# Two norms with their squares summed on VectorE first, and two attention exponentials issued half a chunk later

## The chip, the cores and the metric

The kernel runs on one core of a Trainium2 chip. The metric is the time of one execution on the device in microseconds (us). The engines of the core are TensorE (PE for its matmuls, PEld for its weight loads), VectorE (DVE), ScalarE (ACT), GpSimd (POOL) and SyncE (SP), which here only issues the weights' DMAs. Each engine works through its own list of instructions in order, and they meet at semaphores: an instruction can wait until a semaphore has reached a number, and another raises it when it ends.

## The reference

Two models of width 1024 run one after the other on 256 positions, all in float32. What the change touches is the second (an adaptive-norm block with attention, then one with a short convolution):

```python
def second_block(x, c, ...):                       # cut
    for i in range(2):
        mod = silu(c) @ w_ada[i] + b_ada[i]        # six vectors: shift, scale and gate, twice
        h = rms_norm(x, norm_mix[i]) * (1 + sc_m) + sh_m
        y = moba_attention(h, ...) if i == 0 else short_conv(h, ...)
        x = x + g_m * y
        h = rms_norm(x, norm_ffn[i]) * (1 + sc_f) + sh_f
        x = x + g_f * ((silu(g) * u) @ w_down[i])  # g, u = split(h @ w_gate_up[i])
```

`rms_norm` divides each position by the root of the mean of its 1024 squares (plus 1e-6). The attention has 8 heads of 128 channels; with 256 positions it is plain causal softmax attention, with normed queries and keys.

## The kernel before

The residual stream stands in `res`, transposed: 8 tiles of 128 channels by 256 positions. Every product of a weight and an activation is made of three fast fp32r matmuls (high half by high half, high by low, low by high), in `products` (L1726 to L1728). So each weight unit (128x1024) is first split: ACT copies it rounded to `w_hi` (L597), DVE subtracts to get `w_lo` (L1033), and PE waits for `lo_ready`. Weights come in chunks of two units; the lists of ACT and DVE hold the splits about two chunks ahead of PE's use of them, and between the splits the other work of the stage. The order of all lists is written out by hand in the code; there is no scheduler.

**The second attention** (PE list at c = 0 to 11 for the query, key and value chunks `QKV` + c; c = 12 to 15 are the output projection's chunks `OUT2` + 0 to 3). Beside each half chunk (c, h) stands a piece of the attention, by tables of slots. For head s: PE makes the scores, DVE scales and masks them into `logit2` and takes the negated row maximum `nmax` (`SCORES2`, L1609 to L1613), ACT takes the exponential into `prob2` (L956), DVE multiplies by the reciprocal of the row sum (`weights2`, L1619 and L1621, in DVE's list at the slot of `SCORES2`), PE turns the result over (`PROBS2`, L2224), ACT copies it (L952), and PE multiplies by the values (`VALUES2`, L2235), for which it waits for the copied values too (`v2_ready`, DVE L1632). Also in ACT's list are the squares and the copy of each query or key chunk (`head_squares`, L927 and L929), for which PE's sums of squares wait (`head_sums`, L2204 and L2207), and which wait for the chunk's last matmul.

**The norms before the three up projections** (numbers 1, 3 and 5; before `UP1`, `UP2`, `UP3`, after `OUT1`, `OUT2`, `OUT3`). The last output chunk of the projection runs in two halves on PE: outputs of banks 0 and 1 of four weight rows (then `bank_done`), and the outputs of the other bank, row by row (r = -2, -1, 0, 1). DVE adds the finished banks to `res` (`update`, L1170 and L1178; j = 0 to 3, two tiles each). ACT squares two tiles at a time into `scr` (L606, L621), and PE adds the squares over channels by a plain float32 matmul with ones (`square_part`, L1883): one matmul for each tile, two for each part, parts 0, 1 and 2 between the rows of the last output chunk, parts 3 and 4 in the first up chunk. Meanwhile the first two up chunks already run on the not yet normed activations ("raw", `raw_chunk`, L1797, L1799, L1808), whose two halves ACT (`raw_upper`, L628) and DVE (`raw_lower`, L1124) make. The root of the mean goes through ACT's Ln and Exp (L636, L639) and one Newton step on DVE (L1059 to L1067); the third up chunk (`arriving`, L1763 to L1771) runs on the normed activations (L1072, L650, L1081), and the fourth is the first in steady order.

## Time and profile before

| | us |
|---|---|
| median of 3 runs (lowest, highest) | 910.41 (909.77, 912.11) |
| the profiled execution | 912.87 |
| its span in the trace | 911.3 |
| PE busy | 901.9 (99%) |
| DVE busy | 753.0 (83%) |
| ACT busy | 507.5 (56%) |
| POOL busy | 49.5 (5%) |

The span is the stretch of the trace; the execution's own time is 1.6 us more. A busy share of PE counts matmuls whose ends are modelled and that overlap, so a small wait can hide in it: what PE loses is better seen where two starts in the timeline are further apart than their neighbours. Times in the trace are counted from the start of the span.

### The profile page before, as it was taken

Reading aid. Unit: us, or ns where it says so; the run is one execution under the profiler, and the core shown is the slowest. Engines: PE = TensorE matmul, PEld = TensorE weight load, DVE = VectorE, ACT = ScalarE, POOL = GpSimd, SP = SyncE. Lnnn points to the kernel's source line nnn. Section 1 sums busy time; section 2 is a strip of 40 time slices with the busy share of each in tenths; the row PEclk is TensorE's granted clock in tenths of the full one; section 3 lists DMA queues with packets and bytes.
Section 4 is the critical chain, followed back from the end, with each engine's and each line's share of the span. In section 5 each row is a group of like instructions: output and inputs, shape, how many; then the busy total and the mean of one; then the engine's idle time right before and its main releaser. Section 6 shows DMA issues by size and latency. Waiting matters only on the chain.

```text
span 911.3 us, 18262 instructions
## 1 busy us (share of the span) xinstructions
PE 901.9 (99%) x7351; PEld 877.5 (96%) x7351; DVE 753.0 (83%) x1043; ACT 507.5 (56%) x795; POOL 49.5 (5%) x87
## 2 busy tenths in 40 slices
PE   8999999999999999999999999999999999999998
PEld 8999999999999999999999999999999999999786
DVE  5998989999899799998987887987988887667544
ACT  6456747766665577664754454436554564444531
POOL 5000000000001000010000100100000000000000
PEclk9999999999999999999999999999999999999999
DMA  9887375666667948575379998884677467764541
GB/s 276 288 279 276 106 246 202 215 229 205 230 231 275 327 140 273 171 252 195 127 231 319 323 313 309 314 291 149 201 254 256 135 227 250 239 210 182 184 139 47
DMA packets 132129, 207.72 MB, mean 228 GB/s; under 512 B 4710, under 2 KB 109536, under 8 KB 126944
## 3 DMA queue, kind: packets, MB, share of 16 engines
q1 hardware_dynamic: 123968, 156.47, 51.1%
q0 software_dynamic: 8064, 50.34, 15.9%
q8 instruction: 45, 0.74, 0.3%
q14 instruction: 20, 0.16, 0.1%
q10 hardware_dynamic: 32, 0.01, 0.0%
HBM read 205.75 MB, written 1.05 MB: 227 GB/s over the span
## 4 chain that ended last, share of the span: by engine, by line
PE 86%; DVE 8%; ACT 4%; issue 1%; DMA 1%; SPq 0%; ACTq 0%; DVEq 0%
PE bank L1726 24%; PE bank L1728 24%; PE bank L1727 24%; DVE w_lo L1033 2%; PE bank L1883 2%; PE bank L1799 2%; PE bank L1797 2%; PE bank L1808 2%; PE bank L1771 1%; PE bank L1763 1%; PE bank L1765 1%; ACT w_hi L597 1%; DMA w_raw<-in_w_in 1%; DVE ada_acc L1049 1%; ACT prob L956 1%
## 5 line engine op out<-in xcount | busy, mean ns | idle before, releaser
L1033 DVE TENSOR_TENSOR w_lo<-w_raw,w_hi 128x1024 fp32r<-128x1024 f32 x292 | 351.7, 1221 | 105.7 <-ACT w_hi L597 103.6
L597 ACT ACTIVATE w_hi<-w_raw 128x1024 fp32r<-128x1024 f32 x291 | 304.2, 1056 | 238.2 <-PE bank L1728 220.8
L1726 PE MATMUL bank<-act_hi,w_hi 128*128 128x256 f32 x1296 | 362.2, 279 | 0.1
L1727 PE MATMUL bank<-act_lo,w_hi 128*128 128x256 f32 x1296 | 359.1, 277 | 0.0
L1728 PE MATMUL bank<-act_hi,w_lo 128*128 128x256 f32 x1296 | 359.0, 277 | 0.0
L1727 PEld LDWEIGHTS bank<-act_lo,w_hi 128*128 128x128 f32 x1296 | 244.2, 188 | 0.4 <-issue 0.2
L1726 PEld LDWEIGHTS bank<-act_hi,w_hi 128*128 128x128 f32 x1296 | 243.4, 188 | 0.7 <-issue 0.6
L1728 PEld LDWEIGHTS bank<-act_hi,w_lo 128*128 128x128 f32 x1296 | 243.4, 188 | 0.0
L1049 DVE SCALAR_TENSOR_TENSOR ada_acc<-ada_raw,silu_c,ada_acc 128x2048 f32<-128x2048 f32 (+1 forms) x56 | 114.3, 2041 | 3.6 <-DMA ada_raw<-in_w_ada 3.3
L1726 PE MATMUL bank<-hid_hi,w_hi 128*128 128x256 f32 x352 | 98.2, 279 | 0.0
L1727 PE MATMUL bank<-hid_lo,w_hi 128*128 128x256 f32 x352 | 97.2, 276 | 0.0
L1728 PE MATMUL bank<-hid_hi,w_lo 128*128 128x256 f32 x352 | 97.2, 276 | 0.0
L554 POOL DMA_DIRECT2D ada_raw<-in_w_ada x56 | 29.8, 531 | 737.6 <-DVE ada_acc L1049 730.6
L1726 PEld LDWEIGHTS bank<-hid_hi,w_hi 128*128 128x128 f32 x352 | 66.1, 188 | 0.2
L1727 PEld LDWEIGHTS bank<-hid_lo,w_hi 128*128 128x128 f32 x352 | 66.1, 188 | 0.1
L1728 PEld LDWEIGHTS bank<-hid_hi,w_lo 128*128 128x128 f32 x352 | 66.1, 188 | 0.0
L688 ACT ACTIVATE hid_hi<-hidden 128x512 f32 (+1 forms) x33 | 20.9, 632 | 51.0 <-DVE hidden L1220 49.3
L1726 PE MATMUL bank<-ot_hi,w_hi 128*128 128x256 f32 x128 | 37.4, 292 | 0.0
L1726 PE MATMUL bank<-w_hi,act_hi 128*128 128x256 f32 x128 | 36.9, 288 | 0.0
L1199 DVE SCALAR_TENSOR_TENSOR conv<-bank,vec,conv 128x255 f32<-128x255 f32 (+1 forms) x88 | 35.5, 475 | 0.6 <-ACT conv L668 0.6
L1727 PE MATMUL bank<-w_lo,act_hi 128*128 128x256 f32 x128 | 35.7, 279 | 0.0
L1728 PE MATMUL bank<-w_hi,act_lo 128*128 128x256 f32 x128 | 35.7, 279 | 0.0
(321 smaller groups left out, 1405.5 us busy)
## 6 DMA issues: line engine op xcount, KB each, us to landing
w_raw<-in_w_gate_up SPq DMA_DIRECT2D x44, 1024.0 KB, 5.2
ada_raw<-in_w_ada POOLq DMA_DIRECT2D x40, 1024.0 KB, 5.7
w_raw<-in_w_down SPq DMA_DIRECT2D x33, 1024.0 KB, 6.5
w_raw<-in_w_in SPq DMA_DIRECT2D x23, 1024.0 KB, 6.6
w_raw<-in_w_up SPq DMA_DIRECT2D x22, 1024.0 KB, 5.7
w_raw<-in_w_qkv SPq DMA_DIRECT2D x12, 1024.0 KB, 7.0
w_raw<-in_w_out SPq DMA_DIRECT2D x8, 1024.0 KB, 7.3
ada_raw<-in_w_ada POOLq DMA_DIRECT2D x16, 512.0 KB, 4.5
```

Source lines behind the costliest of these rows:

```text
L554: pool.dma_start(ada_raw[:, j, 0:width], w_ada_2[l][cols(j * P, 2 * P, i, P), s * ADA_W + left:s * ADA_W + left + width]).then_inc(ada_lan ...
L597: act.activation(unit(w_hi, u), raw_half(c, h), ACT.Copy).then_inc(hi_ready, 1)
L688: act.activation(hid_hi[:, cols(2 * p, 4, i, 2), :], hidden[:], ACT.Copy).then_inc(hid_hi_r, 1)
L1033: dve.tensor_tensor(unit(w_lo, u), raw_half(c, h), unit(w_hi, u).bitcast(F32), ALU.subtract).then_inc(lo_ready, 1)
L1049: dve.scalar_tensor_tensor(ada_acc[:, s, part], ada_raw[:, n % 2, 0:width], silu_c[:, k:k + 1], ada_acc[:, s, part], ALU.mult, ALU.add).th ...
L1199: ins = dve.scalar_tensor_tensor(conv[:, q, lag:T], src[:, (q % 2) * T:(q % 2 + 1) * T - lag], vcol(tile, base + f, 4, i), conv[:, q, lag: ...
L1726: pe.matmul(dst, a_hi, b_hi, start=start, stop=False, skip_group_check=True)
L1727: pe.matmul(dst, a_hi, b_lo, start=False, stop=False, skip_group_check=True)
L1728: return pe.matmul(dst, a_lo, b_hi, start=False, stop=stop, skip_group_check=True)
L1797: pe.matmul(dst[t], weights(w_hi, k, t), hi[:, k, 0:width], start=k == 0 and (n > 1 or t == 0), stop=False, skip_group_check=True)
L1799: pe.matmul(dst[t], weights(w_lo, k, t), hi[:, k, 0:width], start=False, stop=False, skip_group_check=True)
L1808: ins = pe.matmul(dst[t], weights(w_hi, k, t), lo[:, k, 0:width], start=False, stop=k == KT - 1, skip_group_check=True)
```

## The change

- For norms 3 and 5, DVE adds the squared tiles before PE sums them: tiles 2 and 3 to tiles 0 and 1, then tiles 4 and 5 to the same (`add_squares`, two 128x512 additions). PE then makes one part of two matmuls in the place of three parts of two; it waits for `sq_added`. Parts 3 and 4 stay.
- ACT squares the three pairs of tiles first and makes most raw upper halves after them.
- DVE's list around these norms: the fold of the modulation for norm 3 (`fold_sum(2)`) and one split of a weight unit stand before the modulation; all eight raw lower halves stand together after the last update; the Newton step takes two instructions on DVE, since ACT makes the mean and the square of the first guess; both splits of the third up chunk stand before the low halves of the normed activations.
- In the second attention ACT takes the exponentials of heads 0 and 3 half a chunk later (`EXPS2`), and at slot (12, 0) its piece of the attention comes before its split.

```diff
+EXPS2 = [(3, 1), (4, 0), (5, 0), (6, 1), (8, 0), (9, 0), (11, 0), (11, 1)]
+PAIRED = (3, 5)
...
                     if raw:
-                        if j == 2 and n not in (2, 4):
+                        if j == 2 and n == 1:
                             split_unit(*late)
...
-                        raw_upper(n, 2 * j)
-                        if (n, j) != (4, 2):
-                            raw_upper(n, 2 * j + 1)
+                        for k in ((), (0,), (1, 2, 3, 4, 5))[j] if n in PAIRED else (2 * j, 2 * j + 1):
+                            if (n, k) != (4, 5):
+                                raw_upper(n, k)
+                            if k == 3 and n in PAIRED:
+                                split_unit(*late)
...
+                if n in PAIRED:
+                    act.activation(n_a[:], bank[SUM_BANK[n]][:, 0:T], ACT.Identity, bias=eps[:], scale=1.0 / D
+                                   ).then_inc(y_mean, 1)
                 act.wait_ge(ln_ready, n)
                 act.activation(n_y[:], n_y[:], ACT.Exp, scale=-0.5).then_inc(y_ready, 1)
+                if n in PAIRED:
+                    act.wait_ge(y_ready, n)
+                    act.activation(n_t[:], n_y[:], ACT.Square).then_inc(y_sq, 1)
...
-                for h in heads_at(SCORES2, c, half):
+                for h in heads_at(EXPS2, c, half):
                     act.wait_ge(m2_ready, h + 1)
...
+                    if (c, h) == (12, 0):
+                        attend2(c, h)
+                        split_unit(QKV + c + 2, h)
+                        continue
...
+            def root(n):
+                if n in PAIRED:
+                    dve.wait_ge(y_mean, PAIRED.index(n) + 1)
+                    dve.wait_ge(y_sq, PAIRED.index(n) + 1)
+                    link(dve.scalar_tensor_tensor(n_t[:], n_t[:], -0.5, n_a[:], ALU.mult, ALU.mult))
+                    link(dve.scalar_tensor_tensor(rstd[:], n_t[:], 1.5, n_y[:], ALU.add, ALU.mult))
+                    return
...
+                if n in PAIRED:
+                    split(c0 + 2)
                 for j in range(4):
-                    if c0 is not None and j % 2 == 0:
+                    if c0 is not None and n not in PAIRED and j % 2 == 0:
                         split_unit(c0 + 2, j // 2)
...
+            def add_up_paired(n, c0, gate, piece):
+                def step(j):
+                    update(bank[OUT_BANKS[c0][j]], j, gate)
+                split_unit(c0 + 4, 0)
+                modulation(piece)
+                dve.wait_ge(unit_done, 2 * (c0 + 2) + 2)
+                step(0)
+                step(1)
+                dve.wait_ge(bank_done, BANKS_DONE[c0] + 1)
+                step(2)
+                add_squares(n, 0)
+                add_squares(n, 1)
+                split_unit(c0 + 4, 1)
+                dve.wait_ge(unit_done, 2 * (c0 + 3) + 2)
+                step(3)
+                raw_lower(n, range(KT))
+                split_unit(c0 + 5, 0)
+
+            def add_squares(n, later_pair):
+                dve.wait_ge(sq_ready, 5 * (n - 1) + 2 + later_pair)
+                if later_pair:
+                    dve.wait_ge(sq_added, 2 * PAIRED.index(n) + 1)
+                pair = slice(2 + 2 * later_pair, 4 + 2 * later_pair)
+                dve.tensor_tensor(scr[:, 0:2, :], scr[:, 0:2, :], scr[:, pair, :], ALU.add).then_inc(sq_added, 1)
...
+                    if (c, h) == (13, 1):
+                        fold_sum(2)
+                        attend2(c, h)
+                        split_unit(QKV + c + 2, h)
+                        continue
...
-            fold_sum(2)
             add_up(OUT2, lambda k: mod[:, 0, G_M + k:G_M + k + 1], 2)
...
-                        if n == 3 and outputs[0] == 2 and r < 1:
+                        if n == 3 and outputs[0] == 2 and r < 1 and NORM_AFTER[c0] not in PAIRED:
                             square_part(NORM_AFTER[c0], r + 2)
+                        if n == 3 and outputs[0] == 2 and r == 0 and NORM_AFTER[c0] in PAIRED:
+                            square_part(NORM_AFTER[c0], 0)
...
-                pe.wait_ge(sq_ready, 5 * (n - 1) + part + 1)
+                if part == 0 and n in PAIRED:
+                    pe.wait_ge(sq_added, 2 * PAIRED.index(n) + 2)
+                else:
+                    pe.wait_ge(sq_ready, 5 * (n - 1) + part + 1)
```

PE's list in the last output chunk of `OUT2`, around the last part of squares ahead of the up projection; first before, then now (`scr` are the squares, `ot_hi` and `ot_lo` the attention's output).

```order
L1728 MATMUL bank<-ot_hi,w_lo 128x256
L1883 MATMUL bank<-scr,ones 128x256 [waits sq_ready]
L1883 MATMUL bank<-scr,ones 128x256
L1726 MATMUL bank<-ot_hi,w_hi 128x256
L1727 MATMUL bank<-ot_lo,w_hi 128x256
```

```order
L1789 MATMUL bank<-ot_hi,w_lo 128x256
L1949 MATMUL bank<-scr,ones 128x256 [waits sq_added]
L1949 MATMUL bank<-scr,ones 128x256
L1787 MATMUL bank<-ot_hi,w_hi 128x256
L1788 MATMUL bank<-ot_lo,w_hi 128x256
```

The place is the same; the two earlier pairs (not shown) are gone, and what this one waits for comes from DVE and no more from ACT.

DVE's list at the same norm, from the second half of the first four updates of `res` on; first before, then now.

```order
L1178 SCALAR_TENSOR_TENSOR res<-bank,mod,res 128x256
L1033 TENSOR_TENSOR w_lo<-w_raw,w_hi 128x1024 [waits hi_ready]
L1178 SCALAR_TENSOR_TENSOR res<-bank,mod,res 128x256 [waits bank_done]
L1178 SCALAR_TENSOR_TENSOR res<-bank,mod,res 128x256
L1033 TENSOR_TENSOR w_lo<-w_raw,w_hi 128x1024 [waits hi_ready]
L1123 TENSOR_TENSOR raw_lo<-mod,raw_hi 128x8x2 [waits raw_hi_r]
L1124 SCALAR_TENSOR_TENSOR raw_lo<-res,gain,raw_hi 128x256
L1124 SCALAR_TENSOR_TENSOR raw_lo<-res,gain,raw_hi 128x256 [waits raw_hi_r] x2
L1033 TENSOR_TENSOR w_lo<-w_raw,w_hi 128x1024 [waits hi_ready]
L1178 SCALAR_TENSOR_TENSOR res<-bank,mod,res 128x256 [waits unit_done]
```

```order
L1235 SCALAR_TENSOR_TENSOR res<-bank,mod,res 128x256 [waits bank_done]
L1235 SCALAR_TENSOR_TENSOR res<-bank,mod,res 128x256
L1221 TENSOR_TENSOR scr<-scr 128x512 [waits sq_ready]
L1221 TENSOR_TENSOR scr<-scr 128x512 [waits sq_added,sq_ready]
L1050 TENSOR_TENSOR w_lo<-w_raw,w_hi 128x1024 [waits hi_ready]
L1235 SCALAR_TENSOR_TENSOR res<-bank,mod,res 128x256 [waits unit_done]
L1235 SCALAR_TENSOR_TENSOR res<-bank,mod,res 128x256
L1152 TENSOR_TENSOR raw_lo<-mod,raw_hi 128x8x2 [waits raw_hi_r]
L1153 SCALAR_TENSOR_TENSOR raw_lo<-res,gain,raw_hi 128x256
L1153 SCALAR_TENSOR_TENSOR raw_lo<-res,gain,raw_hi 128x256 [waits raw_hi_r] x7
```

The split that stood before the `bank_done` updates has gone ahead of the modulation; the two additions follow these updates, and the raw lower halves and one more split now stand behind the last updates.

ACT's list at head 0 of the second attention (chunk 3); first before, then now. `h_sq` and `q` are the squares and the copy of chunk 3, `prob` is the exponential.

```order
L956 ACTIVATE prob,rowsum<-logit,nmax 128x128 [waits m2_ready]
L956 ACTIVATE prob,rowsum<-logit,nmax 128x256
L927 ACTIVATE h_sq<-bank 128x512 [waits qk_ss,unit_done]
L929 ACTIVATE q<-bank 128x512
L597 ACTIVATE w_hi<-w_raw 128x1024 [waits unit_done]
L597 ACTIVATE w_hi<-w_raw 128x1024 [waits unit_done,w_landed3]
```

```order
L940 ACTIVATE h_sq<-bank 128x512 [waits qk_ss,unit_done]
L942 ACTIVATE q<-bank 128x512
L602 ACTIVATE w_hi<-w_raw 128x1024 [waits unit_done]
L969 ACTIVATE prob,rowsum<-logit,nmax 128x128 [waits m2_ready]
L969 ACTIVATE prob,rowsum<-logit,nmax 128x256
L602 ACTIVATE w_hi<-w_raw 128x1024 [waits unit_done,w_landed3]
```

The exponential has moved behind the squares, the copy and one split; head 3 (chunk 6) reads the same. DVE's list is not changed there: its reciprocal for the head stands where it stood.

## Rows read from the trace of the kernel before

**Rows 1.** The page, part 1: busy time of each engine.

```profile
PE 901.9 (99%) x7351; PEld 877.5 (96%) x7351; DVE 753.0 (83%) x1043; ACT 507.5 (56%) x795; POOL 49.5 (5%) x87
```

**Rows 2.** Waits of PE, 350 to 425 us: total, times, longest.

```profile
PE bank L2207 <- ACT q L929: 1.3, 2, 1.1
PE bank L2224 <- ACT prob_t L952: 0.4, 1, 0.4
```

**Rows 3.** Timeline of PE, norm 3: start, length, engine, line, operation, count.

```profile
437.18 0.28 PE L1728 MATMUL bank<-ot_hi,w_lo 128*128 128x256 f32 x1
437.29 0.28 PE L1726 MATMUL bank<-ot_hi,w_hi 128*128 128x256 f32 x1
...
437.86 0.28 PE L1728 MATMUL bank<-ot_hi,w_lo 128*128 128x256 f32 x1
437.98 1.03 PE L1883 MATMUL bank<-scr,ones 128*128 128x256 f32 x4
438.65 0.47 PE L1726 MATMUL bank<-ot_hi,w_hi 128*128 128x256 f32 x1
438.96 0.28 PE L1727 MATMUL bank<-ot_lo,w_hi 128*128 128x256 f32 x1
...
441.12 1.03 PE L1883 MATMUL bank<-scr,ones 128*128 128x256 f32 x4
```

**Rows 4.** The instructions of line 1883, by length in ns (min/median/max).

```profile
L1883 PE MATMUL bank<-scr,ones x64: 377/379/483, 137.5 to 723.7; 128*128 128x256 f32 x64
```

**Rows 5.** Timeline of DVE, norm 3 and the first up chunks.

```profile
438.35 0.87 DVE L1178 SCALAR_TENSOR_TENSOR res<-bank,mod,res 128x256 f32<-128x256 f32 x2
...
457.70 2.36 DVE L1033 TENSOR_TENSOR w_lo<-w_raw,w_hi 128x1024 fp32r<-128x1024 f32 x2
...
464.88 0.69 DVE L1227 TENSOR_TENSOR hid_lo<-hidden,hid_hi 128x512 fp32r<-128x512 f32 x1
```

**Rows 6.** Timeline of ACT, norm 3: the third squaring of two tiles.

```profile
439.31 0.62 ACT L606 ACTIVATE scr<-res 128x512 f32<-128x512 f32 x1
```

**Rows 7.** Timeline of PE: the fourth chunk of the up projection begins.

```profile
460.61 0.28 PE L1726 MATMUL bank<-act_hi,w_hi 128*128 128x256 f32 x1
```

**Rows 8.** Timeline of PE, second attention; the bracket is idle time before and releaser.

```profile
356.06 0.28 PE L1728 MATMUL bank<-w_hi,act_lo 128*128 128x256 f32 x1
357.43 1.05 PE L2207 MATMUL bank<-ones,h_sq 128*128 128x1 f32 x8 [1.10 <-ACT q L929]
...
372.20 1.12 PE L2204 MATMUL bank<-h_sq,ones 128*128 128x512 f32 x2
...
377.51 0.28 PE L1728 MATMUL bank<-act_hi,w_lo 128*128 128x256 f32 x1
...
380.34 0.28 PE L1728 MATMUL bank<-w_hi,act_lo 128*128 128x256 f32 x1
380.87 1.05 PE L2207 MATMUL bank<-ones,h_sq 128*128 128x1 f32 x8 [0.24 <-ACT q L929]
...
388.53 0.67 PE L2235 MATMUL bank<-prob_t,v 128*128 128x256 f32 x2
...
420.85 0.28 PE L1728 MATMUL bank<-ot_hi,w_lo 128*128 128x256 f32 x1
421.48 0.52 PE L2224 MATMUL bank<-ident,prob 128*128 128x128 f32 x3 [0.35 <-ACT prob_t L952]
```

**Rows 9.** Timeline of ACT, second attention.

```profile
355.43 0.41 ACT L956 ACTIVATE prob<-logit,nmax 128x128 f32<-128x128 f32 x1 [2.42 <-DVE nmax L1613]
...
357.28 1.99 ACT L597 ACTIVATE w_hi<-w_raw 128x1024 fp32r<-128x1024 f32 x2
...
371.57 0.58 ACT L929 ACTIVATE k<-bank 128x512 f32<-128x512 f32 x1
...
378.86 0.40 ACT L956 ACTIVATE prob<-logit,nmax 128x128 f32<-128x128 f32 x1 [1.41 <-DVE nmax L1613]
```

**Rows 10.** Timeline of DVE, second attention.

```profile
378.42 0.41 DVE L1613 TENSOR_REDUCE nmax<-logit 128x1 f32<-128x256 f32 x1
379.88 0.17 DVE L1619 RECIPROCAL rinv<-rowsum 128x2 f32<-128x2 f32 x1 [1.05 <-ACT prob L956]
...
387.69 0.69 DVE L1632 COPY v<-bank 128x512 f32<-128x512 f32 x1
```

More of the change, by code:

```diff
@@ L286, in model_kernel @@
         sq_ready = sem("sq_ready")
+        sq_added = sem("sq_added")
         ss_ready = sem("ss_ready")
@@ L1050, in ada @@
                                          ada_acc[:, s, part], ALU.mult, ALU.add).then_inc(ada_used, 1)
-            def norm(n, gain, version, shift=None, c0=None):
+            def root(n):
[5 more added lines that the diff above has]
+                    return
                 dve.wait_ge(ln_ready, n)
@@ L1067, in norm @@
                     link(dve.scalar_tensor_tensor(rstd[:], n_t[:], 1.5, n_y[:], ALU.add, ALU.mult))
+            def norm(n, gain, version, shift=None, c0=None):
+                root(n)
                 def part(k):
@@ L1149, in add_up @@
                 n = NORM_AFTER[c0]
-                if piece is not None:
-                    modulation(piece)
+                if n in PAIRED:
+                    add_up_paired(n, c0, gate, piece)
+                    return
                 for j in range(4):
```

2 lines of the change are left out of this document (added).

## The prediction

> **What bounds the kernel now.** I read the page's busy line first: PE 99%, DVE 83%, ACT 56% [rows 1]. PE sets the end, so a matmul taken off PE is time, and work added to DVE or ACT costs only where PE comes to wait for it. PE's share cannot show small waits, so I then read PE's waits around the changed places [rows 2] and the start times in its timeline [rows 3, 8]. The reader is to see two things. At norm 3 PE never waits: its matmuls follow each other 0.114 us apart (437.18 to 437.29) and the squares stand between them. In the second attention it waits three times for ACT, and each time ACT had been waiting for DVE's row maximum [rows 9]; there the pace is set by a loop of DVE (maximum), ACT (exponential), DVE (reciprocal), in which DVE is hardly ever idle except for that exponential. Last I read DVE's and ACT's timelines at the same places [rows 5, 6, 10] for how late each input would be. All times are of the profiled execution.
>
> **Part 1: four pairs of float32 matmuls less.** One pair: the start at 437.86 and the start at 438.96 are 1.10 us apart; without the squares between, two steps of 0.114 make 0.23. So a pair takes 0.87 us from PE [rows 3]. It includes the slower first matmul after it (438.65, length 0.47). All the squares with ones have one length, 377 to 379 ns in the middle [rows 4], so norm 5 is taken like norm 3. Norm 3 loses two pairs, norm 5 two: 4 x 0.87 = 3.48 us less. Neither this nor the raw products beside them is hidden by another engine.
>
> **Part 2: the wait for the added squares.** The remaining pair now waits for a chain over three engines, in a place that PE reaches 1.74 us sooner: before, the third pair started at 441.12; now PE is there at 439.38. The chain starts with `bank_done`, by the matmul of 437.18, which ends at 437.46. A hand-over between engines costs about 0.05 us in these rows (the maximum ends at 378.83 and the exponential starts at 378.86; the copy of k ends at 372.15 and PE starts at 372.20 [rows 8 to 10]). Step by step: two updates 437.51 to 438.38 (0.87) [rows 5]; the squaring to 439.05 (0.05 + 0.62) [rows 6]; the second addition to 439.79. The trace has no addition of two 128x512 float32 tiles; the nearest row is the subtraction of this size, 0.69 [rows 5], and I take that (bounds: 0.62, the squaring of the same size on ACT, and 0.87, two updates of half the size). The first addition and its 0.6 lie beside the squaring. With 0.05 more PE starts the pair at 439.84 and has waited 0.46, say 0.45. Behind the waiting matmul stand the last products of the chunk and the first raw chunk; all of PE moves with it. Bounds 0.25 (a hand-over of nothing: the chain has four) to 0.8 (addition 0.87, and ACT late by a raw half). Twice: +0.9 us, between 0.5 and 1.6.
>
> The Trainium skill ("Perfetto Trace Analysis", per-instruction lifecycle) says that the end which a profile shows comes before the semaphore update has spread to the other engines, so that part of every hand-over stands in no instruction's window. That speaks against a change that replaces one hand-over by four. The trace agrees and gives it a size, 0.03 to 0.05 each; leaving it out, the wait would be 0.25 and the whole sum 0.4 us better.
>
> **Part 3: what else waits behind the earlier PE.** PE is 1.74 - 0.45 = 1.3 us ahead from here on, and DVE must keep up. The closest unit is the first of the fourth up chunk. Before: DVE starts that split at 457.70 and ends it at 458.9 [rows 5], PE wants it at 460.61 [rows 7], 1.7 to spare. Now DVE loses 1.35 (four instructions of the root become two) and gains 1.2 (the additions), and it waits about 0.1 for the third squares, 0.55 more for the last products before the last updates, and 0.5 for ACT's half of the split that was brought forward. It began at 437.51 and not 438.35, since one split has gone ahead. 458.9 - 0.84 - 1.35 + 1.2 + 0.1 + 0.55 + 0.5 = 459.1, and PE wants it at 460.61 - 1.3 = 459.3. So I cost this at nothing, but with 0.2 to spare; if that cover is gone, each 0.1 us by which DVE is later costs 0.1 at each norm. Bounds 0 to 0.5 at each. The Identity and Square that ACT takes over lie before DVE's arrival at the root and cost nothing; moving the raw upper halves behind the squares only serves part 2; the eight raw lower halves in one run end before the raw chunk's last third, which wants them. The fold of the modulation fills a wait that DVE had for ACT; PE still makes its matmul in the same place. SP's and POOL's lists are the same, and no weight is wanted sooner than its lead of two chunks.
>
> **Part 4: the exponentials.** Head 0: chunk 3's last matmul ends about 353.6, so ACT makes squares, copy and one split (0.95) by 355.6, and only then the exponential, which before started at 355.43 [rows 9]: DVE is 0.15 to 0.35 later. PE's wait at 357.43 goes; the gap there was 1.37 against 0.11, so 1.26 is offered [rows 8]. But it is not kept: the next hand-overs to PE come through the DVE loop. At 372.20 PE starts 0.05 after the copy of k, which stands behind the exponential of head 2 in ACT's list and so behind DVE's maximum. By there PE is no longer early but 0.2 late. Head 3: chunk 6's last matmul starts at 377.51 and ends at 377.79; squares, copy and split follow, 0.47 + 0.47 + 0.95, and the exponential starts about 379.9 in place of 378.86 [rows 8, 9]. DVE already waits at this reciprocal (1.05 idle [rows 10]), so it is late by a full 1.0 from 379.88 on. From there to 388.3 DVE's timeline has no idle time, and the copy of the values ends at 388.38, 0.15 before PE starts the product with them at 388.53 [rows 8, 10]. So PE's wait at 380.87 (0.4) goes, and at 388.53 one of about 0.95 comes. At 421.48 the copy before the split takes away a wait that widened the step from 0.11 to 0.63; an ordinary step into such a turn is about 0.1, so 0.4 is really gained. Net: +0.95 - 0.4 = +0.55 us. Bounds -1.9 (all three waits gone, 1.1 + 0.4 + 0.4, and nothing in their place) and +1.1 (the last one stays). I take the walk and not the middle, since it rests on rows at each step.
>
> **Sum.** -3.48 + 0.9 + 0.55 = -2.03 us. The profiled execution's own time, 912.87 (span 911.3), would be 910.8; from the median, 910.41, it is 908.4, 0.22% less.
>
> **Rivals.**
> - *The waits are smaller than walked.* The additions come in time, or DVE makes up for the late exponential before PE wants the copied values. For it: the copy ends 0.15 before PE's start, so a little of the delay is free; against: DVE shows no idle time for 8 us after head 3. Without the attention's cost alone: -2.6, 907.8. With the waits at `sq_added` at their lower bound too: -3.0, 907.4. With all three of the attention's waits simply gone: -3.48 + 0.9 - 1.9 = -4.5, 905.9.
> - *DVE becomes the bound after the norms* (the side of slower). The place is the fourth up chunk, where 0.2 us is left. Both splits of the third chunk, 2.3 us, now stand before the low halves; if these come through late, or ACT's half for the second split comes a table load later, PE waits. The price is 1 to 1 for each norm; it decides between the signs when both norms lose over 1.0 us. With one run of two splits, 2.3, at each: -2.03 + 4.6 = +2.6, 913.0. Against it: DVE's work between the updates and this place is the same within 0.2 us.
> - *The change doesn't do what it says*, that is, PE's matmuls for the squares go but the time doesn't, since PE would have waited there for the raw halves: then the gain of part 1 is 0 and the time 911.9. Against: PE's start times show no wait in the raw chunk before, and the raw halves come no later relative to PE.
>
> **Chances.** My forecast 0.58; smaller waits 0.30; DVE the bound, or no gain from the matmuls, 0.12. A change of less than 0.3% (2.7 us) can hardly be told from none here. Of the first case nearly all lies within 0.3%; of the second two thirds are beyond it (below 907.7) and some of the first; of the third, half are slower by over 0.3%. So: faster 0.30, within 0.3% 0.64, slower 0.06. The range reaches from between the better cases to just over the time before: 906.4 to 910.8. The forecast's own range is 907.4 to 909.4.
>
> **What would show it.** In the profile after: 48 records in the group of the squares with ones in place of 64; PE steps of 0.114 where two pairs stood; an idle time of 0.3 to 0.6 before the pair that is left, released by DVE's addition; no wait before PE's sums for chunks 3 and 6, DVE's idle time before the reciprocal of head 3 grown from 1.05 to about 2, and a wait of 0.8 to 1.0 before the product with the values of head 2, released by DVE's copy. The prediction is wrong if PE shows a wait in the third or fourth up chunk, or if DVE's wait for the exponential of head 3 does not grow.

## The result, and the profile after

| | before | after |
|---|---|---|
| median of 8 runs each (lowest, highest), us | 910.08 (909.30, 912.11) | 914.16 (913.40, 914.56) |
| after / before | | 1.0038, 95% interval 1.0029 to 1.0048 |
| the profiled execution, and its span, us | 912.87, 911.3 | 914.56, 913.0 |

The kernel became 4.1 us slower; forecast were 2 us less. Nothing in the page shows it. The page after, parts 1 and 2 in lines, against [rows 1]:

```profile
PE 902.5 (99%) x7335; PEld 878.2 (96%) x7335; DVE 753.3 (83%) x1043; ACT 507.9 (56%) x799; POOL 49.6 (5%) x87
...
PEclk9999999999999999999999999999999999999999
```

PE has 16 records of matmuls less, as meant (8 matmuls; a plain float32 matmul leaves two records), and is busy 0.6 us longer. So I looked for where two places with the same work between them have moved apart. Three places stand in both traces: the first product of the third chunk behind norms 3, 4 and 5 (in UP2, IN3 and UP3), and PE's last product. The view by windows, before and then after, cut at these moments; columns: window, length, then busy time (and instructions) of PE, PEld, DVE, ACT and POOL, the granted clock, the DMA share and GB/s:

```profile
455.15:639.48 184.33, 184.33 (x1605) 183.64 (x1603) 152.82 (x159) 92.91 (x116) 13.15 (x20) 1.00 0.82 280
639.48:734.08 94.60, 94.60 (x790) 93.68 (x789) 81.98 (x123) 51.77 (x78) 3.16 (x6) 1.00 0.65 212
734.08:906.98 172.90, 172.90 (x1248) 160.85 (x1246) 107.76 (x124) 77.73 (x90) 3.17 (x6) 1.00 0.54 184
```

```profile
454.09:644.58 190.49, 190.49 (x1604) 189.79 (x1603) 154.46 (x163) 93.72 (x116) 13.18 (x20) 1.00 0.79 270
644.58:735.74 91.16, 90.83 (x782) 89.93 (x781) 80.31 (x119) 51.22 (x80) 3.18 (x6) 1.00 0.66 220
735.74:908.66 172.92, 172.92 (x1247) 160.87 (x1246) 109.56 (x128) 78.79 (x90) 3.18 (x6) 1.00 0.55 184
```

The first row is the loss: up and down projection of the second block, which the change does not touch, take 190.49 us for 184.33, with the same 1602 matmuls (by their start times; the view also counts those that reach into the window) and no idle time of PE. The second is 3.44 shorter, of which norm 5 can explain 1.2. PE was at the third chunk of UP2 at 454.09, 1.06 before where it was, of which 0.43 was there before the second attention already. To see what 6 us are lost on, I count matmuls in windows that lie wholly inside a steady stretch. Before, then after:

```profile
500.00:600.00 100.00, 100.00 (x884) 100.00 (x884) 85.54 (x66) 47.02 (x52) 10.51 (x15) 1.00 0.90 314
650.00:700.00 50.00, 50.00 (x427) 50.00 (x426) 43.03 (x51) 25.01 (x32) 3.16 (x6) 1.00 0.78 256
```

```profile
500.00:600.00 100.00, 100.00 (x851) 100.00 (x850) 81.58 (x64) 46.06 (x51) 10.00 (x14) 1.00 0.87 306
650.00:700.00 50.00, 50.00 (x444) 50.00 (x443) 43.92 (x53) 25.19 (x34) 3.18 (x6) 1.00 0.77 257
```

The same 128x256 matmuls come 884 or 851 to 100 us. **The stream has two paces**, one start each 0.1133 us or each 0.1178 us (means over the start times), 4.5 ns apart, at a granted clock of 1.00 in all four windows. The view by lines of PE (560 to 600 us, before and after) shows it too: one matmul has a mean length of 276 ns before and 281 after.

```profile
L1726 PE MATMUL bank<-hid_hi,w_hi 128*128 128x256 f32 x106 | 29.3, 276 | 0.0
```

```profile
L1787 PE MATMUL bank<-hid_hi,w_hi 128*128 128x256 f32 x93 | 26.1, 281 | 0.0
```

In the trace after, 1391 steps in a row are of the long kind, from 454.09 to the fold's matmul at 617.9: 1391 x 4.5 ns = 6.3 us. In the trace before, it is 510 steps from 641.6 to the fold's matmul at 701.7, 2.3 us, which the trace after does not have. Between the two profiled executions, 912.87 and 914.56, this makes 6.3 - 2.3, less 2.0 for the changed places, near the 1.7 that lie between them. Most executions of the kernel before lie about 2.3 us lower, so against the medians it is 6.3 - 2.0 = 4.3, for 4.1 measured; the changed places themselves came out about as forecast. PE and DVE around norm 3 after, for [rows 3, 5]; the bracket is idle time and its releaser:

```profile
439.36 0.28 PE L1789 MATMUL bank<-ot_hi,w_lo 128*128 128x256 f32 x1
439.95 1.13 PE L1949 MATMUL bank<-scr,ones 128*128 128x256 f32 x4 [0.32 <-DVE scr L1221]
440.73 0.47 PE L1787 MATMUL bank<-ot_hi,w_hi 128*128 128x256 f32 x1
```

```profile
435.90 2.60 DVE L1235 SCALAR_TENSOR_TENSOR res<-bank,mod,res 128x256 f32<-128x256 f32 x6
438.43 1.48 DVE L1221 TENSOR_TENSOR scr<-scr 128x512 f32<-128x512 f32 x2
```

The step from 439.36 to the pair at 439.95 is 0.60 in place of 0.12, and from the pair to the next product it is 0.78 (439.95 to 440.73) where it was 0.67 (437.98 to 438.65 [rows 3]). So the wait costs 0.48 in front of the pair and 0.10 behind it. The squares with ones are 48 for [rows 4], with the same lengths:

```profile
L1949 PE MATMUL bank<-scr,ones x48: 377/379/483, 137.0 to 725.4; 128*128 128x256 f32 x48
```

In the second attention the wait for chunk 3's sums is gone, DVE's idle time before the reciprocal of head 3 has grown from 1.05 to 1.93, and PE waits for the copied values [rows 8, 10]. First the DVE row, then PE's waits of the whole execution:

```profile
380.45 0.17 DVE L1676 RECIPROCAL rinv<-rowsum 128x2 f32<-128x2 f32 x1 [1.93 <-ACT prob L969]
```

```profile
PE bank L2301 <- DVE v L1689: 1.1, 1, 1.1
...
PE bank L2290 <- DVE prob L1678: 0.9, 2, 0.8
PE bank L1949 <- DVE scr L1221: 0.7, 2, 0.3
...
PE bank L2270 <- ACT k L942: 0.4, 1, 0.4
```

So the experiments ask one thing first: what puts a stretch into the long step? There are three long stretches of 128x256 matmuls behind the norms: UP2 with DOWN2 (about 1390 steps, worth 6.3 us), IN3 with OUT3 (510, 2.3 us), and UP3 with DOWN3 (910 to 960, 4.1 to 4.3 us).

### The profile page after: what moved, and what is told of

Same layout as the page of the kernel before. It is cut to its first block, busy times and chain, and to the rows that moved or that the text cites. A ratio compares the mean times of both kernels' runs of the same rounds, so it can differ in the third digit from the quotient of the medians.

```text
span 913.0 us, 18236 instructions
## 1 busy us (share of the span) xinstructions
PE 902.5 (99%) x7335; PEld 878.2 (96%) x7335; DVE 753.3 (83%) x1043; ACT 507.9 (56%) x799; POOL 49.6 (5%) x87
## 3 DMA queue, kind: packets, MB, share of 16 engines
HBM read 205.75 MB, written 1.05 MB: 227 GB/s over the span
## 4 chain that ended last, share of the span: by engine, by line
PE 86%; DVE 9%; ACT 3%; issue 1%; DMA 1%; SPq 0%; DVEq 0%; ACTq 0%
PE bank L1787 24%; PE bank L1789 24%; PE bank L1788 24%; DVE w_lo L1050 2%; PE bank L1860 2%; PE bank L1858 2%; PE bank L1869 2%; PE bank L1949 2%; PE bank L1832 1%; PE bank L1824 1%; PE bank L1826 1%; ACT w_hi L602 1%; DVE ada_acc L1066 1%; ACT prob L969 1%; DMA x_in<-in_x 1%
```

## The experiments

Line numbers are those of each kernel. Each kernel ran 11 to 13 times beside the kernel before, which ran 35, 35 and 29 times in the three sets (medians 910.20, 910.52 and 911.00). In all of them the times stand in groups. In the 99 executions of the kernel before, 70 lie at 911.1 or below and 29 between 911.5 and 913.9. Only one execution of each kernel has a trace, so the assignment of the other executions to stretches is by the distances between the groups, not read from their steps. These distances leave one thing open: UP2 alone (6.3) and IN3 with UP3 (2.3 + 4.1 = 6.4) look alike. The three sets ran on three chips (that of the first result is not on record), so a kernel is compared with the kernel before of its own set.

**Set 1.** The probe of e1 and e2 is one more fp32 matmul of one column, which adds zeros (two records in the trace):

```diff
+            def nudge(dst):
+                pe.matmul(dst[:, 0:1], ones[:], before[:, 0, 0:1], start=False, stop=False, skip_group_check=True)
...
+                    if operand in NUDGED and k == 5:
+                        nudge(dst)
```

*e1, the changed kernel, probe in UP2.* 

> The changed kernel with one more fp32 matmul of one column (ones times a column of zeros, added to the open bank, so nothing changes in the result) in the third up chunk, the one after the two raw chunks, behind its high tile 5. Reading to test: in the second feed-forward part every 128x256 matmul starts 0.1178 us after the one before, where the kernel before has 0.1133; 1391 of them in a row, 6.3 us, with no wait between. Theory A (the pace is a state of TensorE that a restart sets by its exact moment, and that stays until the stream is next interrupted by an fp32 matmul or a wait): from the added matmul on the steps are 0.1133, the stretch gives back 6.1 us less some 0.5 for the two switches, median 908.5 us, between 907.5 and 909.5. Theory B (the pace is set by what the other engines do beside it, which the change reordered): the steps stay at 0.1178 and the kernel is 0.4 to 0.6 slower, 914.7 us.

Measured: the profiled execution took 907.75, the stretch in UP2 is at the short step. The 13 executions: 907.75, ten from 911.92 to 913.14, two at 914.22 and 914.66; median 912.51, ratio 1.0027 [1.0017, 1.0036]. The trace, at the probe (L1817), and the count for the stretch:

```profile
455.81 0.28 PE L1830 MATMUL bank<-act_hi,w_lo 128*128 128x256 f32 x1
455.93 0.28 PE L1817 MATMUL bank<-before,ones 128*128 128x1 f32 x2
456.07 0.36 PE L1828 MATMUL bank<-act_hi,w_hi 128*128 128x256 f32 x1
456.27 0.28 PE L1830 MATMUL bank<-act_hi,w_lo 128*128 128x256 f32 x1
...
500.00:600.00 100.00, 100.00 (x885) 100.00 (x884) 84.93 (x66) 47.22 (x51) 10.55 (x15) 1.00 0.89 313
```

From 455.81 to 456.27 are 0.46 us where two steps would take 0.23, so a probe costs 0.23, 0.25 with the three longer steps behind it. But the stretch was at the short step from 453.7 on, before the probe at 455.9, so this trace does not show that the probe ends the long one; it shows that the stretch can be short with every engine's order as changed. Up to the probe e1 is the changed kernel, instruction for instruction, and the changed kernel's own trace has this stretch long: one program takes either step. That speaks against theory B. The traced execution is the only one of the 13 at its time, so it is not a typical one. My median was wrong by 4.0: 912.5 is 907.75 plus 4.7, near the price of UP3's stretch, which the changed kernel had at the short step; no trace of those executions shows it.

*e2, the kernel before, probe in IN3.* 

> The kernel before with the same one-column fp32 matmul in the second block's input projection (IN3), third chunk, behind its high tile 5, just after the two gaps of 0.187 and 0.221 us from which on its trace shows 510 steps of 0.1178 us (641.6 to 701.7). Theory A: the steps behind it fall to 0.1133, 2.3 us less some 0.5: 1.8 us under the kernel before if the timed runs of that kernel have the slow stretch as its profiled one has. Theory B: no step changes, 0.5 us slower. If the timed runs of the kernel before mostly do not have this stretch (its profiled execution was its slowest, 912.11 against a median of 910.08), the gain is less, down to a loss of 0.5.

(The profiled execution of the kernel before took 912.87, not 912.11, a little above all 8 others.) Measured: 910.66, ratio 1.0003 [0.9994, 1.0012], no execution above 911.28. Against the kernel before in the same set: its upper group (911.7 to 913.1, 5 of 35) is missing, and e2's median stands 0.7 above that of the lower one (909.96), where a probe costs 0.25; the rest is not explained. The stretch in IN3 is at the short step in the trace (442 in 650 to 700 us, 427 before). The gain I expected was computed from a profiled execution that is one of the rarer, longer ones.

*e3, the attention part alone.*

```diff
-PAIRED = (3, 5)
+PAIRED = ()
...
-                        if j == 2 and n == 1:
+                        if j == 2 and n not in PAIRED + (2, 4):
...
+                if piece is not None:
+                    modulation(piece)
```

> The kernel before with the attention part of the change alone: the later exponentials (EXPS2), attend2 ahead of the split at (12, 0) and (13, 1), the fold's sum earlier; norms 3 and 5 as before with three pairs of squares ahead and after. The prediction's term is +0.55 us; the traces of the two kernels show +0.9, +0.5, +0.3 and +1.2 at four waits and less at others. Theory A: whatever is lost beyond about 1 us is pace, to be seen as stretches of 0.1178 us steps that the kernel before does not have; median 910.5 to 911.5 if the long stretches fall as in the kernel before, 6 more if the feed-forward stretch falls slow. Theory B (the pairing of the squares and its new DVE order slows the stretch behind norm 3): the stretch from the third up chunk on is at 0.1133 here.

Measured: 910.69, ratio 1.0007 [0.9998, 1.0017]: eight executions from 909.73 to 910.81 and four from 912.07 to 912.63, the profiled one (912.10) among these, with IN3 at the long step (x427) and UP2 at the short one. As expected of both theories; it doesn't tell them apart.

*e4, the paired norms alone.* ACT's attention piece at (12, 0) and the fold's sum also stand where they stood.

```diff
+EXPS2 = SCORES2
...
-                    if (c, h) == (12, 0):
-                        attend2(c, h)
...
-                    if (c, h) == (13, 1):
-                        fold_sum(2)
-                        attend2(c, h)
...
+            fold_sum(2)
```

> The changed kernel with the attention part undone: exponentials where the scores are, both splits ahead of attend2, the fold's sum behind the loop; the paired norms 3 and 5 stay. By the prediction's terms this is -3.48 + 0.9 = -2.6 us against the kernel before at one pace: 907.5. Theory A: TensorE comes to the third up chunk at another moment than in the changed kernel, so the feed-forward stretch may fall to 0.1133 (median 907 to 908.5) or stay at 0.1178 (913 to 914.5), and the trace's steps say which. Theory B (the paired norm's DVE order is the cause): 0.1178 there for certain, 913 to 914.5.

Measured: six executions from 911.64 to 913.22 and six from 918.88 to 920.63, ratio 1.0065 [1.0041, 1.0089]. One and the same program stands in two groups 7 us apart. The profiled one, 911.90, has UP2 short and UP3 long:

```profile
500.00:600.00 100.00, 100.00 (x885) 100.00 (x884) 85.01 (x66) 47.16 (x51) 10.51 (x15) 1.00 0.89 312
650.00:700.00 50.00, 50.00 (x441) 49.78 (x441) 43.04 (x49) 26.46 (x33) 3.17 (x6) 1.00 0.80 264
745.00:845.00 100.00, 100.00 (x839) 99.32 (x839) 66.41 (x65) 46.09 (x53) 3.17 (x6) 1.00 0.65 220
```

Theory B, that the paired norm's DVE order makes UP2 long for certain, has fallen: the order is in this kernel, and UP2 is short. PE came into UP3's third chunk at the short step and went long only 48 matmuls later, at the first product of the fourth chunk: DVE's split for it ends at 734.28, PE starts at 734.44, and the steps there are 0.118, 0.121 and 0.120, with no idle time in any view. Both theories' times were off, since I had left UP3's stretch out of account.

**Set 2: the same probe at all three places, behind the last low tile's wait** (`k == 7`), in four kernels, to take the stretches out of the comparison.

```diff
+NUDGED = (3, 4, 5)
...
                     pe.wait_ge(h_lo, 4 * operand + k // 2 + 1)
+                    if operand in NUDGED and k == 7:
+                        nudge(dst)
```

*e5, the changed kernel.* 

> The changed kernel with the one-column fp32 matmul at three places: in the third chunk of UP2, IN3 and UP3, behind the wait for its last low tile (h_lo), ahead of tile 7's low products. One of them cost 0.25 us in the traces of the two kernels that have it. Theory A (a restart after an fp32 matmul relaxes to 0.1133 us, so no long stretch is slow in any execution): 914.16 - 6.3 + 0.75 = 908.6 us, and the executions within 1.5 us of each other. Theory B (the added matmul is only a new throw of the dice, as any interruption is): executions in groups 2.3, 4.1 and 6.2 us above the lowest, median anywhere from 908.6 to 915.

*e6, the kernel before, with these lines.* 

> The kernel before with the same three matmuls at the same places. Theory A: its lower group of times (35 executions, the lowest 909.13, most between 909.3 and 910.6) plus 0.75, 910.3 us, and the group at 912.5 to 913.1 gone. Theory B: the group about 2.3 us higher stays. Against e5, at one pace in both, this is what the change itself is worth: 2.0 us by the prediction's sum, e5 under e6.

*e7, e3 with these lines.* 

> The attention part alone with the three added matmuls: against e6 the prediction says +0.55 us (910.9); the waits counted in the two traces let 0.3 to 1.0 appear. Rival: the attention part is worth more than 1 us, since four waits of 0.3 to 1.2 us are new in the trace of the changed kernel, and carries the loss.

*e8, e4 with these lines.* 

> The paired norms 3 and 5 alone (attention as before) with the three added matmuls: against e6 the prediction says -3.48 + 0.9 = -2.6 us (907.7). Rival: the paired norms themselves cost, by DVE's splits ahead of the low halves or by what follows sq_added, and the time is not under e6. Theory A of the pace says one group of times within 1.5 us here, where the same kernel without the added matmuls had 911.6 to 913.2 in six executions and 918.9 to 920.6 in six.

| | median (lowest, highest), us | ratio to the kernel before | against e6 |
|---|---|---|---|
| e6, before | 910.83 (909.94, 911.86) | 1.0004 [0.9994, 1.0014] | |
| e7, attention alone | 911.27 (910.66, 911.83) | 1.0001 [0.9992, 1.0010] | +0.44 |
| e8, norms alone | 909.39 (908.50, 911.49) | 0.9980 [0.9971, 0.9989] | -1.44 |
| e5, all of the change | 908.98 (907.98, 911.31) | 0.9981 [0.9971, 0.9990] | -1.85 |

In all four traces all three stretches are at the short step behind the probe, and the groups are gone: 44 of 46 executions lie within 2.0 us of their kernel's lowest (one of e5 and one of e8 are 3.0 to 3.3 above theirs). The probe not only stands in stretches that are short anyway. In three of the twelve places PE came to it in long steps and left it in short ones: UP3 in e5 (46 steps ahead) and in e8 (46), IN3 in e8 (29). In e5, by windows of 5 us ahead of and behind the probe at 734.75:

```profile
729.50:734.50 5.00, 5.00 (x44) 5.00 (x44) 5.00 (x10) 3.07 (x4) 0.00 (x0) 1.00 0.56 177
736.00:741.00 5.00, 5.00 (x46) 5.00 (x45) 4.93 (x10) 3.20 (x5) 0.00 (x0) 1.00 0.65 216
```

So theory A holds as far as these runs go, with one limit: after other interruptions than this one the outcome is open. e5 is faster than both kernels, and against e6 the change is worth 1.85 us by the medians, with the forecast at 2.03. From the start times of the same places as above, in us, each trace for itself:

| stretch | e6 | e7 | e8 | e5 |
|---|---|---|---|---|
| third chunk behind norm 2 to that of UP2 (attention, norm 3) | 122.55 | 122.98 | 122.48 (see below) | 121.89 |
| to that of IN3 | 184.57 | 184.58 | 184.58 | 184.59 |
| to that of UP3 (norm 5) | 92.61 | 92.60 | 91.51 | 91.39 |
| to the last product | 173.17 | 173.14 | 173.33 | 173.33 |

By these four rows together e5 is 1.70 under e6. With the steps equal, the stretch that had lost 6.16 us is the same to 0.02 in all four. Norm 5 gains 1.1 to 1.2 (my terms: 1.29; the 0.10 behind the waiting pair was not in them). The attention part alone costs 0.43 (0.55), and norm 3 together with it gains 0.66 (0.74).

Norm 3 alone can't be read from e8, since its trace has a stretch at another clock. The view by windows, e8 and then e6 at the same place (the granted clock is the third number from the end):

```profile
357.00:360.00 3.00, 3.00 (x13) 2.71 (x13) 3.00 (x4) 1.90 (x6) 0.00 (x0) 0.50 0.15 47
```

```profile
357.00:360.00 3.00, 3.00 (x25) 2.90 (x26) 2.93 (x5) 2.80 (x7) 0.00 (x0) 1.00 0.51 164
```

PE had been idle for 1.0 us there, had made the eight one-column sums of squares of chunk 3 and begun the scores; then the granted clock fell to 0.50, the 1.2 GHz level, and its matmuls came 0.21 us apart. It fell 1.6 us behind e4, which has the same instructions up to UP2's third chunk, and was still 0.83 behind at 388. In e4, at full clock, this stretch took 121.65, against 122.56, 122.44 and 122.54 in the traces of the kernel before, e2 and e6. So norm 3 alone gains 0.8 to 0.9.

That and the attention's -0.43 would make about 0.4, where the two together gained 0.66: they are not independent. In e8 PE waits for the added squares 0.7 in place of 0.3, and so it does in e4:

```profile
PE bank L1947 <- DVE scr L1218: 0.7, 1, 0.7
```

The fold's sum, which the attention part moves forward, stands in both right ahead of the updates. That this is the reason was not tried by itself.

The clock also shows in the medians. Of the 146 timed executions of the kernels with the exponentials where they were (the kernel before, e2, e4, e6, e8) 77 have a mean granted clock of 0.998 or less, of the 92 with the later exponentials 3. In e8's trace such a mean, 0.998, is the one stretch above. In the lower group of the kernel before these executions stand 0.87, 0.85 and 1.21 us above the others of their set. So the later exponentials seem to save, in about half of the executions, some 0.9 us that the sum never counted; no experiment was made on it, and only e8's execution has a trace. Among executions at 0.999 or more alone, e5 stands 1.5 us under e6 (10 and 6 executions), e8 1.3 under it (5) and e7 0.9 over it (11). The clock does not make the groups 2.3 us and more apart: executions at 1.00 stand in both of them (e3: 910.28 and 912.63).

**Set 3: how the stretch falls long.**

*e9, the changed kernel with one probe in the second raw chunk.*

```diff
+                    if n == 3 and not arrives and k == 3:
+                        pe.matmul(dst[0][:, 0:1], ones[:], before[:, 0, 0:1], start=False, stop=False, skip_group_check=True)
```

> The changed kernel with one one-column fp32 matmul in the second raw chunk of UP2, ahead of low tile 3, ten 258-column matmuls before the first 256-column one of the third chunk, where the slow stretch began in the trace of the changed kernel (454.1). Nothing else moves but TensorE's time, 0.2 to 0.3 us. Theory A1 (whether the stretch goes slow depends on the exact moment and phase in which TensorE enters it): not all executions are slow any more, the times stand in two groups, 908.0 to 909.5 and 914 to 915, and the median is under 914.2. Theory A2 (something fixed beside the third chunk of the changed kernel makes it slow, whatever the phase): all executions stay at 913.6 to 915.

Measured: 913.56, ratio 1.0021 [1.0008, 1.0033]; six executions from 912.00 to 912.82 and six from 914.31 to 915.29. The trace of one of the latter:

```profile
453.09 0.28 PE L1869 MATMUL bank<-before,ones 128*128 128x1 f32 x2
453.23 1.45 PE L1871 MATMUL bank<-raw_lo,w_hi 128*128 128x258 f32 x10
454.51 0.29 PE L1824 MATMUL bank<-act_hi,w_hi 128*128 128x256 f32 x1
...
500.00:600.00 100.00, 100.00 (x885) 100.00 (x884) 84.90 (x67) 47.17 (x51) 10.52 (x15) 1.00 0.89 313
650.00:700.00 50.00, 50.00 (x427) 50.00 (x427) 42.99 (x50) 25.63 (x32) 3.17 (x6) 1.00 0.78 256
745.00:845.00 100.00, 100.00 (x852) 100.00 (x851) 66.76 (x65) 46.14 (x54) 3.17 (x6) 1.00 0.66 221
```

A quarter of a us, 1.4 us ahead of the stretch, turned all three in this execution: UP2 is now short, IN3 and UP3 are long, where the changed kernel had long, short, short. The distance between the groups (2.3) and the whole (about 908.5 + 4.3 = 912.8, + 2.3 = 915.1) fit UP2 short and UP3 long in all twelve, IN3 long in six; for the upper group UP2 alone long (914.8) would fit as well, except for the traced one. Theory A2 would need a fixed cause beside UP2's third chunk, and in this trace all of that was still there and the stretch was short. Neither group is where I had put it, for UP3's sake again.

*e10, the changed kernel with DVE's two splits back between the low halves.*

```diff
-                if n in PAIRED:
-                    split(c0 + 2)
...
-                    if c0 is not None and n not in PAIRED and j % 2 == 0:
+                    if c0 is not None and j % 2 == 0:
```

> The changed kernel with the two splits of the third up chunk's next weights back between DVE's low halves in norms 3 and 5 (as in the kernel before), all else as changed. Theory A2: DVE's two splits ahead of the low halves are what the slow stretch hangs on; with the order back the stretch is at 0.1133, median 908.0. Theory A1: TensorE enters the third chunk as in the changed kernel, since no wait of it hangs on this order up to there, so the stretch is slow in all or nearly all executions, 913.5 to 915.

Measured: five executions from 908.14 to 910.47, five from 914.55 to 915.28, two at 919.16 and 919.53; median 914.55, ratio 1.0023 [0.9997, 1.0049]. The profiled one, 908.49, has all three stretches short in the windows. Neither theory had this: the order is not what the long stretch hangs on (seven of twelve times stand 6 us and more above the lowest), but nor is the outcome kept. The trace says why. As theory A1 has it, PE came into UP2's third chunk at the long step, as in the changed kernel (and into UP3's too). After 15 steps it had to wait for the second split of the chunk, which the order put back makes late. PE, then the split on DVE, which ends at 455.46:

```profile
455.14 0.28 PE L1824 MATMUL bank<-act_hi,w_lo 128*128 128x256 f32 x1
455.51 0.38 PE L1822 MATMUL bank<-act_hi,w_hi 128*128 128x256 f32 x1
```

```profile
454.24 1.22 DVE L1050 TENSOR_TENSOR w_lo<-w_raw,w_hi 128x1024 fp32r<-128x1024 f32 x1
```

The step is 0.37 in place of 0.12, and behind this interruption the stream went to the short step. So this edit is not one without a wait, as its expectation took it to be: it adds one more restart in each up projection, and the outcome of that one differs from execution to execution. It also shows what the two early splits of the change are for: with PE earlier, the old order costs it 0.25 us.

*e11, the changed kernel with probes in UP2 and UP3 only.*

```diff
-NUDGED = (3, 4, 5)
+NUDGED = (3, 5)
```

> The changed kernel with the one-column fp32 matmul in the third chunk of UP2 and UP3 only, not in IN3. The three of e5 gave 908.98. If IN3's stretch stays fast without one, as in the changed kernel's trace, 0.25 us less, 908.7; if it falls slow in some executions, these stand 2.3 us higher and the median is 909 to 911.

Measured: 909.00, ratio 0.9979 [0.9967, 0.9990]: eight executions from 907.87 to 909.23 and four from 910.09 to 911.41, the profiled one (910.89) among these, with IN3 long (x427). The second branch of the expectation holds. The ratio to the kernel before is that of e5 (0.9979 and 0.9981), and the spread is larger.

**All traces together.** Every one of the 13 profiled executions can be put together from the same pieces (S short step, L long step, in UP2, IN3 and UP3; the last column is the time less 6.3, 2.3 and 4.1 for its long ones, estimates from the counts above):

| | stretches | us | less the long steps |
|---|---|---|---|
| before | S L S | 912.87 | 910.6 |
| e2, e6 (with probes) | S S S | 909.98, 910.83 | the same |
| e3, e7 | S L S, S S S | 912.10, 910.66 | 909.8, 910.7 |
| after | L S S | 914.56 | 908.3 |
| e1, e5, e8, e10 | S S S | 907.75, 908.63, 908.90, 908.49 | the same |
| e4, e9, e11 | S S L, S L L, S L S | 911.90, 915.29, 910.89 | 907.8, 908.9, 908.6 |

Kernels without the paired norms end at 909.8 to 910.8, those with them at 907.8 to 908.9.

**Where a long stretch begins.** The start times of the 13 traces show one thing more. Ahead of each of the three stretches PE runs the raw chunks, whose 258-column matmuls repeat a pattern of eight steps, 0.118 to 0.125 us. Of the 39 entries into a third chunk (13 traces; UP2, IN3, UP3), 33 came 0.119 or 0.120 us after the last raw matmul and began short, and six came 0.125 after it and began long: UP2 in the changed kernel and in e10, UP3 in e5, e8, e9 and e10. The same six are those in which the products right behind the pair of squares that waits for `sq_added` had run at the long step (in the changed kernel 0.118 a step from 441.04 on, in e1 0.114 from 440.15 on). That wait stands in 16 of the 39 places; in the 23 where the squares do not wait for an addition, no entry was long. So the wait that the change puts in front of the squares is itself one more restart, and how it falls goes on through the raw chunks into the up projection. This is read across traces; no run has the change without that wait. The other long stretches begin later: IN3's (and a short one in e8) behind a wait 16 matmuls into the third chunk that all kernels have, e4's in UP3 at the fourth chunk.

## Why the prediction was wrong

- **Part 1 (four pairs less, 3.48 us) and part 2 (the wait, 0.9 us): right in kind, the wait a little too small.** The pair stands 0.48 to 0.49 us later than an ordinary step would put it at each norm, for 0.45, and the way behind it is 0.10 longer, which the prediction did not have: 1.2 us for 0.9. The last hand-over, from DVE's addition (438.43 + 1.48 = 439.91) to PE (439.95), took 0.04, within the 0.03 to 0.05 that the prediction set. At equal steps norm 5 gained 1.1 to 1.2 us and norm 3 with the attention part 0.66.
- **Part 3 (DVE keeps up with the third and fourth chunk): right, with nothing in hand.** The views show no wait of PE in either. But at norm 5 of the changed kernel DVE's split for the fourth chunk ends at 741.05 and PE starts there at 741.21, with steps of 0.117, 0.124 and 0.122 around it, and in e1 one step there is 0.136. The cost is 0.02 us at most; in e4 this is the very place where UP3's stretch went long. So the rival in which DVE becomes the bound has fallen, although the measured time is close to the 913.0 it gave. Its agreement was chance.
- **Part 4 (the attention, +0.55): right in size, not in all places.** At the values 1.08 us idle for 0.95, at 421.48 the wait is gone, and DVE's idle time is 1.93 for "about 2". The whole part cost 0.43 in the traces of e6 and e7. Not foreseen: PE waits 0.75 for the first turned result at 364.8, and the later exponentials seem to spare many executions a fall of the granted clock.
- **The sum: the step that failed.** It adds terms of the changed places and takes all else as it was: I read a step of 0.114 us at norm 3 in the first view, used it for what a removed pair leaves behind, and took for granted that the stretches behind the norms keep theirs. They do not, and the change itself puts a new restart, the wait for the added squares, ahead of two of them. The stretch from 454.09 to 617.9 went from 0.1133 to 0.1178 us a step, +6.3 us, and this one term is three times the sum of all others. -2.03 + 6.3 = +4.3 us, and +4.1 is what was measured (910.08 to 914.16).
- **The base.** The profiled execution of the kernel before, from which the sum was made, held 2.3 us of long steps in IN3 that most of its executions do not have. It stood 2.5 us above the median, and the prediction named the difference and did not ask what it was. The counts of [rows 2, 3] could not show it; the counts in equal windows of that same trace (442 or 427 matmuls in 50 us) would have.

What stays open: what in TensorE makes the two steps, and what sets how a restart falls. The runs show that a stretch takes one step and mostly keeps it over hundreds of matmuls, that the same program takes one or the other from execution to execution, and that a few tenths of a us ahead of it change the odds. In the changed kernel's trace the long step was there behind the waiting squares already. Its 8 executions (913.40 to 914.56) fit UP2 long in all of them, but only one has a trace, and why it would be all was not settled.

## What to carry to other kernels

Where one engine is busy 99% of the time with the same instruction, count its instructions in equal windows of both traces before looking for waits: a change of pace by 4% leaves no idle time and no releaser, and outweighs the eight removed matmuls. Compare variants at equal pace (here by one cheap instruction at the head of each long stretch in both), since otherwise a term of 1 us is measured together with a throw of 6. Look at the granted clock of each trace by windows as well, before two traces are subtracted: a mean of 0.998 hid 1.6 us at one place here. And a new wait on the busiest engine had two prices here: its idle time, and how the stream went on behind it. And look at the single times, not the median alone: groups at fixed distances say that a state, and not the edit, is being measured.

## What the runs showed of the hardware

- A stream of 128x256 fp32r matmuls, each with its own weight load, runs at 0.1133 or 0.1178 us a step at a granted clock of 1.00, and mostly keeps its step until a wait or an fp32 matmul interrupts it. At the start of another weight chunk it changed a few times without idle time (from 0.118 to 0.113 at 362.2 in the kernel before, the other way at 734.4 in e4). After most interruptions up to five steps of 0.114 to 0.124 come first; then the stream drops to 0.1133 or stays at 0.1178. Two gaps that look alike went different ways: behind 0.187 and 0.221 us at 641.2 in the kernel before it stayed long for 510 steps, behind 0.191 and 0.222 at 646.3 in the changed one it was short after four:

```profile
641.19 0.28 PE L1765 MATMUL bank<-act_hi,w_lo 128*128 128x256 f32 x1
641.38 0.38 PE L1763 MATMUL bank<-act_hi,w_hi 128*128 128x256 f32 x1
641.60 0.28 PE L1765 MATMUL bank<-act_hi,w_lo 128*128 128x256 f32 x1
```

```profile
646.30 0.28 PE L1826 MATMUL bank<-act_hi,w_lo 128*128 128x256 f32 x1
646.49 0.39 PE L1824 MATMUL bank<-act_hi,w_hi 128*128 128x256 f32 x1
646.71 0.28 PE L1826 MATMUL bank<-act_hi,w_lo 128*128 128x256 f32 x1
```

- Behind the one-column fp32 matmul, all 16 restarts in the traces of e1, e2, e5 to e8 and e11 went to the short step, three of them out of a long stretch. Behind the transposes of the two attentions, in the traces of both kernels and of e1 to e4, the stream was long at the next interruption in 42 of 90 restarts, most of them some 23 steps long (0.1 us, less than a probe costs).
- 258-column fp32r matmuls repeat steps of 0.119, 0.120, 0.123, 0.120, 0.122, 0.118, 0.120 and 0.125 us, a mean of 0.121.
- In the trace of e8 the granted clock was 0.50 (1.2 GHz) from 357 to 360 us, right behind 1.0 us without a matmul and eight one-column ones. The traces of the kernel before, e2, e4 and e6 have the same idle time at that place, and the clock stayed at 1.00.
- The Trainium skill ("TensorE: Matmul & The Clock Gate", Back-to-back issue gap) gives one fixed addition per matmul for the warm array, and says that in a stream of weight loads and matmuls both set the spacing. Both steps measured here, 0.1133 and 0.1178 us, are longer than its value for a lone matmul of 256 columns (262 cycles, 0.109 us at 2.4 GHz), and that there are two of them it does not say.
